# First feed-forward output of a hybrid layer in other shapes: sample tokens as 512 streamed columns, prompt tokens by rows

## The reference, cut to what matters

```python
def _swiglu(h, w_in, w_out):
    a, b = jnp.split(h @ w_in, 2, axis=-1)
    return (jax.nn.silu(a) * b) @ w_out
...
    h = _rmsnorm(x, norm_ffn1) * (1 + sc1) + sh1
    x = x + 0.5 * gt1 * _swiglu(h, w_ffn1_in, w_ffn1_out)
    h = _rmsnorm(x, norm_mix) * (1 + sc2) + sh2
```

## Time and profile before

| what | us |
|---|---|
| median of 3 runs | 1291.9 (1290.95 to 1295.19) |
| the profiled execution, its own time | 1289.45 |
| its span | 1287.7 |
| PE busy | 1271.0 |
| DVE busy | 925.0 |
| ACT busy | 553.3 |

### The profile page before, as it was taken

One profiled execution on the slowest core, in us unless ns is written; L12 is line 12 of the kernel. 1 busy time (PEld: TensorE's weight loads), 2 busy tenths in 40 slices (PEclk: granted clock), 3 DMA queues, 4 the chain that ended last, 5 costly groups with the idle time before them and its releaser, 6 DMA issues.

```text
span 1287.7 us, 23042 instructions
## 1 busy us (share of the span) xinstructions
PE 1271.0 (99%) x8861; PEld 1221.2 (95%) x8861; DVE 925.0 (72%) x1537; ACT 553.3 (43%) x920; POOL 97.3 (8%) x81
## 2 busy tenths in 40 slices
PE   8999999999999999999999999999999999999998
PEld 7889999999999999999999899999999999988886
DVE  5668887787887874667789867558988877771424
ACT  6514543445532224664433554346544443551223
POOL 0000000000000000002423663000000000000000
PEclk9999999999999999999999999999999999999999
DMA  9771423232476745248963552242243523274222
GB/s 373 297 269 31 117 79 98 67 96 63 142 213 186 219 128 142 83 119 194 275 186 90 149 156 82 67 77 72 66 130 100 143 68 98 65 186 105 69 82 98
DMA packets 238101, 170.02 MB, mean 132 GB/s; under 512 B 46305, under 2 KB 209606, under 8 KB 236998
## 3 DMA queue, kind: packets, MB, share of 16 engines
q1 hardware_dynamic: 234964, 165.51, 43.3%
q0 software_dynamic: 1440, 2.62, 1.4%
q10 hardware_dynamic: 1618, 0.81, 0.2%
HBM read 154.32 MB, written 19.83 MB: 135 GB/s over the span
## 4 chain that ended last, share of the span: by engine, by line
PE 87%; DVE 8%; ACT 2%; DMA 1%; issue 1%; SPq 0%; DVEq 0%; ACTq 0%
PE ps L1043 33%; PE ps L850 30%; PE ps L1472 11%; PE ps L1419 3%; PE ps L973 1%; PE ps L1405 1%; DMA w_raw<-in_w_ffn_in 1%; DVE w_lo L2108 1%; DVE sub_tmp L2632 1%; PE ps L1198 1%; DVE cv L2512 1%; PE ps L1185 1%; DVE pn L2177 1%; PE ps L918 1%; PE ps L1298 1%
## 5 line engine op out<-in xcount | busy, mean ns | idle before, releaser
L1511 ACT ACTIVATE w_hi<-w_raw 128x1024 fp32r<-128x1024 f32 (+1 forms) x101 | 105.1, 1041 | 312.2 <-PE ps L850 167.6
L2108 DVE TENSOR_TENSOR w_lo<-w_raw,w_hi 128x1024 fp32r<-128x1024 f32 (+1 forms) x101 | 124.2, 1230 | 127.9 <-ACT w_hi L1511 125.8
L850 PE MATMUL ps<-h_hi,w_hi 128*128 128x320 f32 x736 | 171.9, 315 | 0.7 <-DVE w_lo L2108 0.6
L850 PE MATMUL ps<-h_lo,w_hi 128*128 128x320 f32 x736 | 169.5, 311 | 0.0
L850 PE MATMUL ps<-h_hi,w_lo 128*128 128x320 f32 x736 | 169.2, 311 | 0.0
L850 PEld LDWEIGHTS ps<-h_hi,w_hi 128*128 128x128 f32 x736 | 123.7, 189 | 5.1 <-issue 4.8
L1043 PE MATMUL ps<-T_hi,S_hi 128*128 128x320 f32 x408 | 126.0, 309 | 0.0
L1043 PE MATMUL ps<-T_hi,S_lo 128*128 128x320 f32 x408 | 126.0, 309 | 0.0
L1043 PE MATMUL ps<-T_lo,S_hi 128*128 128x320 f32 x408 | 125.9, 309 | 0.0
L850 PEld LDWEIGHTS ps<-h_hi,w_lo 128*128 128x128 f32 x736 | 124.6, 189 | 0.0
L850 PEld LDWEIGHTS ps<-h_lo,w_hi 128*128 128x128 f32 x736 | 124.3, 189 | 0.0
(11 more groups left out here) (391 smaller groups left out, 2889.8 us busy)
## 6 DMA issues: line engine op xcount, KB each, us to landing
w_raw<-in_w_ffn_in SPq DMA_DIRECT2D x50, 512.0 KB, 4.7
cw_raw<-in_w_ada SPq DMA_DIRECT2D x40, 512.0 KB, 4.3
w_more<-in_w_ffn_in SPq DMA_DIRECT2D x34, 512.0 KB, 4.9
ada_w<-in_w_ada SPq DMA_DIRECT2D x16, 1024.0 KB, 8.8
w_raw<-in_w_ffn_out SPq DMA_DIRECT2D x30, 512.0 KB, 3.9
w_raw<-in_w_mix_in SPq DMA_DIRECT2D x28, 512.0 KB, 4.5
w_raw<-in_w_ffn_out SPq DMA_DIRECT2D x16, 448.0 KB, 4.0
w_raw<-in_w_mix_out SPq DMA_DIRECT2D x8, 512.0 KB, 4.0
```

The costliest lines, as they stand in the source:

```text
L850: last = pe.matmul(to[a_slot][b], w, m[:, k0 + k, part[b]], start=start and k == 0 and n == 0, stop=stop and k == kt - 1 and n == 2)
L1511: nc.scalar.activation(w_hi[:, slot, 0:kt * P], w_raw[:, slot, 0:kt * P], ACT.Copy).then_inc(hi_ready, 1)
L2108: nc.vector.tensor_tensor(w_lo[:, slot, 0:kt * P], w_raw[:, slot, 0:kt * P], w_hi[:, slot, 0:kt * P].bitcast(F32), ALU.subtract).then_inc( ...
```

## The change

The output stage works in units of two blocks k by 512 channels (22 units of 1024 columns of weight each; UPC = 11 units for each half c of the channels). Within a unit five parts follow each other, six matmuls each: four tiles of 128 channels, in which the weight is stationary and the 512 sample tokens stream, and part 4, in which g of the 128 prompt tokens is stationary and 512 columns of weight stream. So five PSUM banks fill at once during eleven units, and each half c finishes four tiles of x together. There are 22 x 5 x 6 = 660 matmuls, all 512 wide.

The prompt result comes out with tokens on the partitions. ACT copies it to sa (`copy_prompt`), PE turns it back in four transposes (`turn_prompt`, placed inside the last unit of each half, behind parts 4, 0 and 1), and DVE adds it (`residual_prompt`). The modulation's PSUM banks move to ps2 and ps3. The weights of `load_out_columns` come as two pieces of 512 floats for each partition instead of seven or eight of 128. The same `slot_of` table is kept, but it is read with q + 1, so that a row of a slot follows the split of one unit earlier at the same slot.

```diff
-KO = ((0, 8), (8, 15), (15, 22))
...
+UPC = KF // 2
+U_MI = U_F1O + 2 * UPC
...
+O1_TILE, O1_PROMPT, O1_ADAP, O1_ADAT = ((4, 5, 6, 7), (0, 4, 5, 6)), (0, 1), 2, 3
...
+                sp.dma_start(w_raw[:, slot, 0:kt * width].rearrange("p (k f) -> p k f", k=kt),
...
-                for q in range(3 * KD):
-                    k0, k1 = KO[q % 3]
-                    load_w(u0 + q, q % 2, src[:, k0:k1, P * (q // 3):P * (q // 3) + P], k1 - k0)
+                for q in range(2 * UPC):
+                    c, i = divmod(q, UPC)
+                    load_w(u0 + q, q % 2, src[:, 2 * i:2 * i + 2, OW * c:OW * c + OW], 2, OW)
...
-                        if slot_of[n - 2] == divmod(q - 3, 3):
+                        if slot_of[n - 2] == divmod(q - 2, 3):
...
-            def swiglu_out(u0, a0, g0, g_hi, g_lo, before=lambda j: None, after=lambda j: None, upto=KD):
-                for j in range(upto):
-                    s = j % 2
-                    before(j)
-                    acc_wait(a0 // 2 + j // 2, s)
-                    for b, (k0, k1) in enumerate(KO):
-                        unit(u0 + 3 * j + b, (3 * j + b) % 2, k1 - k0, g_hi, g_lo, s, start=b == 0, stop=b == 2, k0=k0,
-                             h_wait=(lambda k, k0=k0: (g_rdy, g0 + k0 + k + 1)) if j == 0 else None, wide=False)
-                    after(j)
...
+            def first_rows(q, part):
+                c, i = divmod(q, UPC)
+                for k in range(2):
+                    if c == 0:
+                        pe.wait_ge(g_rdy, 2 * i + k + 1)
+                    gh, gl = g2_hi[:, 2 * i + k, :], g2_lo[:, 2 * i + k, :]
+                    wh, wl = (w[:, q % 2, OW * k:OW * k + OW] for w in (w_hi, w_lo))
+                    for n, (g, w) in enumerate(((gh, wh), (gl, wh), (gh, wl))):
+                        start, stop = i == 0 and k == 0 and n == 0, i == UPC - 1 and k == 1 and n == 2
+                        if part < 4:
+                            last = pe.matmul(ps[O1_TILE[c][part]][:, :], w[:, P * part:P * part + P], g[:, TP:T],
+                                             start=start, stop=stop)
+                        else:
+                            last = pe.matmul(ps[O1_PROMPT[c]][:, :], g[:, 0:TP], w, start=start, stop=stop)
+                return last
+            def turn_prompt(c):
+                pe.wait_ge(pt_copied, c + 1)
+                for b in range(4):
+                    last = pe.transpose(ps[O1_PROMPT[c]][:, b * P:b * P + P], sa[:, b * P:b * P + P], ident[:, :])
+                last.then_inc(pt_turned, 1)
+            turn_rows = lambda n: ada_turn(n, 2, cw_r, ps[O1_ADAT])
+            rows_of = lambda c: column_rows(c, ps[O1_ADAP])
+            behind = {7: lambda: rows_of(1), 10: lambda: turn_rows(5), 13: lambda: rows_of(2),
+                      16: lambda: (turn_rows(6), rows_of(3)), 19: lambda: (turn_rows(7), rows_of(4))}
+            for ready in (c11_rdy, u2_rdy, c21_rdy, c12_rdy):
+                pe.wait_ge(*ready(SE[0] - 2))
+            for q in range(2 * UPC):
+                c, i = divmod(q, UPC)
+                ends = i == UPC - 1
+                pe.wait_ge(lo_ready, U_F1O + q + 1)
+                for n, part in enumerate((4, 0, 1, 2, 3) if q > 0 else (0, 1, 2, 3, 4)):
+                    if q == 0 and part == 4:
+                        pe.wait_ge(*c11_rdy(SE[0] - 1))
+                    if q == UPC and part == 4:
+                        pe.wait_ge(*u2_rdy(SE[0] - 1))
+                    if q == UPC and part < 4:
+                        pe.wait_ge(x_upd, max(part, 1))
+                    last = first_rows(q, part)
+                    if ends and n < 4:
+                        last.then_inc(o1_done, 1)
+                    if ends and n == 2:
+                        turn_prompt(c)
+                last.then_inc(mm_done, 1)
+                if q == 7:
+                    pe.wait_ge(*c21_rdy(SE[0] - 1))
+                    pe.wait_ge(*c12_rdy(SE[0] - 1))
+                if q in behind:
+                    behind[q]()
+            pe.wait_ge(x_upd, 4)
+            ada_turn(8, 2, cw_r)
...
-                k0, k1 = KO[q % 3] if q < 3 * KD and u0 == U_F1O else (0, KD)
-                split_hi(u0 + q, q % 2, k1 - k0, (u0 + q) // 2)
+                split_hi(u0 + q, q % 2, KD, (u0 + q) // 2)
...
-                if j < KEPT or j == KD - 1:
+                if j != KEPT:
                     gained_hi(1, j)
-                elif j == KD - 2:
-                    for k in range(KEPT, KD - 1):
...
+            def copy_prompt(c):
+                act.wait_ge(o1_done, 4 * c + 1)
+                if c == 1:
+                    act.wait_ge(ssq_rdy, 4)
+                nc.scalar.activation(sa[:, 0:OW], ps[O1_PROMPT[c]][:, :], ACT.Copy).then_inc(pt_copied, 1)
+            for q in range(2 * UPC):
+                slot = divmod(q + 1, 3)
+                if q > 1:
+                    split_out(U_F1O, q + 1)
+                if q in (8, 14, 17, 20):
+                    ada_out({8: 5, 14: 6, 17: 7, 20: 8}[q], 256, cw_r, ps[O1_ADAP])
+                if q == 1:
                     column_first(1)
...
+                for group in range(2, 5):
+                    if slot_of[KD * group] == slot:
+                        column_first(group)
+                if q == 20:
+                    gained_hi(1, KEPT)
+                if UPC <= q < UPC + 4:
+                    after_ffn1(q - UPC)
+                if q % UPC == UPC - 1:
+                    copy_prompt(q // UPC)
+            for j in range(4, KD - 1):
+                after_ffn1(j)
...
+            def residual_prompt(c):
+                dve.wait_ge(pt_turned, c + 1)
+                if c == 0:
+                    dve.wait_ge(gain_rdy, 4)
+                for b in range(4):
+                    j = 4 * c + b
+                    nc.vector.scalar_tensor_tensor(out=x[:, j, 0:TP], in0=ps[O1_PROMPT[c]][:, b * P:b * P + P],
+                                                   scalar=gate[:, 0, j, 0:1], in1=x[:, j, 0:TP], op0=ALU.mult, op1=ALU.add)
+            def residual_tile(j):
+                c, b = divmod(j, 4)
+                if b < 3:
+                    dve.wait_ge(o1_done, 4 * c + 2 + b)
+                else:
+                    dve.wait_ge(mm_done, U_F1O + UPC * (c + 1))
+                nc.vector.scalar_tensor_tensor(out=x[:, j, TP:T], in0=ps[O1_TILE[c][b]][:, :], scalar=gate[:, 0, j, 1:2],
+                                               in1=x[:, j, TP:T], op0=ALU.mult, op1=ALU.add).then_inc(x_upd, 1)
+                dve.wait_ge(x_upd, j + 1)
+                dve.sem_inc(acc_free[0 if j in (0, 1, 2, 4) else 1], 1)
...
+            for q in range(2 * UPC):
+                slot = divmod(q + 1, 3)
+                if q > 1:
+                    split_out(U_F1O, q + 1)
+                if q in (11, 17, 20):
+                    n = {11: 5, 17: 6, 20: 7}[q]
+                    ada_cols(n, 8 * n, 2, ps[O1_ADAT])
                     dve.wait_ge(mod_rdy, n + 1)
...
+                    if n == 5:
                         gates(1)
...
+                    if n == 7:
                         gains(2)
                         dve.wait_ge(ada_mm, 21)
                         link(shift_columns(1))
                 for n in range(KD, 5 * KD):
...
+                    if n % KD > 0 and slot_of[n] == slot:
                         column_sum(n)
...
+                if q == 20:
+                    gained_lo(1, KEPT)
+                if UPC <= q < UPC + 4:
+                    after_ffn1(q - UPC)
+                if q == UPC - 1:
+                    residual_prompt(0)
+                    for j in range(4):
+                        residual_tile(j)
+            residual_prompt(1)
+            residual_tile(4)
+            for j in range(5, KD):
+                residual_tile(j)
+                after_ffn1(j - 1)
```

More of the change, by code:

```diff
@@ L392, in hybrid_layer @@
         gain_rdy = sem("gain_rdy")
+        o1_done, pt_copied, pt_turned = sem("o1_done"), sem("pt_copied"), sem("pt_turned")
         def seq(engine):
@@ L940, in quarter_step, with ada_turn @@
                 last.then_inc(ada_mm, 1)
-            def ada_turn(n, blocks, src=ada_r):
+            def ada_turn(n, blocks, src=ada_r, to=adat):
                 pe.wait_ge(ada_row, n + 1)
@@ L955, in column_rows @@
                     for g in range(4):
-                        last = pe.matmul(adap[32 * g:32 * g + 32, 0:256], pick[:, 1 - i:33 - i],
+                        last = pe.matmul(to[32 * g:32 * g + 32, 0:256], pick[:, 1 - i:33 - i],
                                          acc_of(c)[:, i, g * 256:(g + 1) * 256], start=i == 0, stop=i == 1)
@@ L1751, in _ @@
             strassen(0)
-            def swiglu_out(u0, n0, more, x0, after, skip=0, upto=KD, aside=lambda j, b: None):
-                for j in range(upto):
-                    if j >= skip:
-                        split_out(u0, 3 * j + 1)
-                    aside(j, 0)
-                    if j > 0:
```

(52 more changed lines are left out.)

36 lines of the change are left out of this document (7 added, 29 removed).

## The result

| | median us | lowest to highest | executions |
|---|---|---|---|
| before | 1292.58 | 1288.75 to 1295.87 | 6 |
| changed | 1302.95 | 1299.88 to 1303.83 | 6 |

The ratio is estimated at 1.007, with a 95% interval of 1.0051 to 1.0089: slower by 9.0 us (6.6 to 11.5). The two medians themselves lie 10.4 us apart. The direction is the one predicted. The predicted time, 1297.7, is 5.3 us too low, and the result lies outside the range of 1293 to 1301. The profiled execution took 1303.5 us, its span is 1301.7, 14.0 us more than the first profile of before.

The account below looks back on a forecast made before the run. The prediction took PE, busy 99% of the span, as the bound. It summed -5.3 - 1.0 - 1.1 + 0.9 + 8.3 + 1.5 + 2.5 = +5.8 us, on the median 1291.9 giving 1297.7 us, range 1293.0 to 1301.0.

Parts of the forecast that it names:

- matmuls, 660 at 226.7 ns: PE, output stage: 1056 matmuls of 146.7 ns become 660 of 226.7 ns, 154.9 to 149.6 us, -5.3 us.
- unit borders: PE, output stage: 0.95 us left over, about 0.12 for each column tile, goes away; -1.0 us (bounds 0 and -1.0).
- old wait: PE's 1.1 us wait on the way from row 24 to a split is replaced by the larger wait; -1.1 us.
- eight transposes: PE turning the prompt result back: four transposes take 0.45 us, twice; +0.9 us.
- wait for the copy: PE before the first four transposes waits 7.8 to 8.9 us for ACT's copy, queued behind row 24's passes; +8.3 us.
- clock: PE's granted clock falls in the idle time and rises as slowly as it fell, 3.0 us at half rate; +1.5 us.
- waits for h6 and h7: Mixer's first unit: PE waits 0.6 and 1.9 us for its input h of tiles 6 and 7; +2.5 us.
- R4: Rival, output stage: stationary-weight sample parts run no denser, weight loading sets the pace; -5.3 becomes 0, 1303.0 us; chance 0.02.
- R1: Rival, ACT between unit 11's split and the copy: copy isn't held up, kernel faster, -4.0 us, 1287.9; chance 0.08.
- R2: Rival, PE's copy wait: it comes but the clock costs nothing (+4.3, 1296.2), or the load is quick (1294.8); chance 0.22.
- R3: Rival, PE's copy wait: row 24 lands after 5.7 us and the clock's rise costs 3.0; +8.2, 1300.1 us; chance 0.15.
- later stages shift by the same amount, since PE stays the bound: Behind the output stage and the mixer's first unit: everything later moves by the same amount, with no further term.

Follow-up runs that it names:

- the second comparison: The unedited changed kernel timed once more against the kernel before: median 1302.3 us, ratio 1.0077 (1.0054 to 1.0099).
- the late PE: The kernel before with 19 extra matmuls (8.1 us, result overwritten) on PE ahead of the mixer's first unit: median 1302.3 us, ratio 1.0074.

## Why the prediction failed, point by point

| step | predicted | measured |
|---|---|---|
| matmuls, 660 at 226.7 ns | -5.3 | -5.3 (L1107 starts 227 ns apart) |
| unit borders | -1.0 | +0.5 |
| old wait | -1.1 | -1.2 |
| eight transposes | +0.9 | +0.7 |
| wait for the copy | +8.3 | +8.1 |
| clock | +1.5 | +2.2 |
| waits for h6 and h7 | +2.5 | +2.9 |
| sum up to the mixer's second unit | +5.8 | +7.9 |

The measured column is PE's distances of starts in the two profiles (for the clock, the slow transposes and matmuls less the same number at full clock); the borders are what remains of the stage's 5.0: 0.2 us at the first matmuls behind the prompt's transposes, the rest hundredths of a us spread over the 660 matmuls. The stage of before has 160.8 to 162.0 in three profiles, so the remainder is good to some 0.6 us.

- *Right:* the sign, the wait, its place, its cause and its size. Taking its cause away took 9.9 us from the stage. The density is right too: R4 and R1 are refuted, and of R2 neither half came (the load took 4.46, and the clock cost 2.2).
- *Mis-sized, the borders:* "-1.0 (bounds 0 and -1.0)". The 0.95 us that I had spread over the column tiles wasn't at tile borders. In the first profile of before, distances clearly above 146.7 ns for a matmul stand only beside the foldings, the modulation's transposes and the wait of 1.1 us: eight places of 0.08 to 0.11 us, 0.8 in all. Where one column tile follows another without such work there is no gap. The change keeps the foldings and the modulation's transposes (at 433.44 us in the changed kernel the first matmul behind a folding is still 0.35 us from the next, not 0.23), so there was nothing to save.
- *Mis-sized, the clock:* "a rise as slow as the fall" made 3.0 us at half rate. The rise took 4.7. R3 had this half right, and not the longer load. The page of the Trainium skill, "TensorE: Matmul & The Clock Gate", section "HAM oscillation — how this bites in real kernels", says that a wait is paid a second time by slow work; the row of 1.12 and 4.45 us agrees, and so does the kernel in which PE was kept busy.
- *The step that failed,* "later stages shift by the same amount, since PE stays the bound", and with it a median that was to lie 2.45 us above the profiled execution for both kernels (the changed kernel's lies 0.55 below its own). PE isn't the bound alone: behind it stands POOL's line. It was in time in the one execution that I read (DVE's products were done at 621.3, PE took them at 622.4), late by 2.7 us in the next one of the same kernel, and late by 1.9 and 1.5 us in the two of the changed kernel. A difference of two profiles, and a median worked out from one, carry that scatter. A range made from one profile's rows had no place for it.

Counted by the stage the answer is 1291.9 + 7.9 = 1299.8, inside the range. The median was missed by 5.3 us: 2.1 us are the mis-sized terms of the sum (7.9 against 5.8), 0.7 the median of the kernel before (1292.58 in six executions, 1291.9 in the three that I had), and 2.5 lie behind the mixer's first unit. By the ratios the time behind that unit is 9.0 less 7.9 and, in the second comparison, 0.0077 x 1292.9 = 10.0 less 7.9, so 1 to 2 us. These are **not settled**. Part can be the longer wait for kg. Another candidate is the low clock behind the waits for h6 and h7, which cost 2.9 us in one trace and 1.4 in another and nothing in three others with the same two waits; how often it comes in the executions without a trace is not known.

## What to carry to other kernels

Where a new consumer on the bottleneck engine takes a value from a side engine, walk that engine's queue back to the last instruction ahead of it that waits for a transfer; one line of program order was worth 9.9 us of the stage here, more than the whole change gives. Short waits of PE in a row are to be priced with the clock too. And before a sum of 6 us is set against a time, look at a second profile of the same kernel: the one read here was 2.5 to 3.5 us under the medians of its kernel, and one line that happened to be short in it made nearly all of its distance to the second.

## What the runs showed of the hardware that was not expected

- Two waits of 0.73 and 1.64 us, with 2.8 us between the starts behind them, were followed by a granted clock of 0.50 in one kernel and by 1.00 in others with the same two waits. In the kernel before, one of 2.7 us was followed by 0.61 and 0.54 in the next windows, and with the late PE one of 2.9 us by 1.00.
- A round of two accumulating transfers of 256 KB took 7.4 to 8.8 us in one execution, with the same size and order each time.
- DVE's split slows down beside POOL's products. In the changed kernel it takes 1.23 us alone and 4.66 while POOL's four products run from 620.7 to 626.3 (DVE's timeline):

```profile
606.72 1.23 DVE L2135 TENSOR_TENSOR w_lo<-w_raw,w_hi 128x1024 fp32r<-128x1024 f32 x1 [0.26 <-ACT w_hi L1540]
...
622.77 4.66 DVE L2135 TENSOR_TENSOR w_lo<-w_raw,w_hi 128x1024 fp32r<-128x1024 f32 x1 [0.26 <-ACT w_hi L1540]
```
